# The expert stage of a two-block transformer kernel as one flat stream of weight pieces

## The chip, the cores and the metric

One core of a Trainium2 chip runs the whole program. The metric is the device time of one execution in microseconds (us), taken as the median of several executions.

## What is computed

Two stacked blocks on 256 tokens of width 1024 (x is 1 x 256 x 1024, float32). The first has two hybrid attention layers, the second has two hybrid mixers (a gated convolution and a delta rule), one behind each a feed-forward part: a dense SwiGLU of width 2816 after the first mixer, and a mixture of experts after the second. The change touches the mixture of experts alone:

```python
def moe_swiglu(x, router_w, w_gate, w_up, w_down):
    logits = (x @ router_w).astype(jnp.float32)
    top_v, top_i = lax.top_k(logits, TOP_K)              # TOP_K = 2 of N_EXPERTS = 8
    gates = jax.nn.softmax(top_v, axis=-1)
    combine = jnp.sum(jax.nn.one_hot(top_i, N_EXPERTS) * gates[..., None], axis=-2)
    y = jnp.zeros_like(x)
    for e in range(N_EXPERTS):
        y = y + combine[..., e:e + 1] * swiglu(x, w_gate[e], w_up[e], w_down[e])
    return y                                             # swiglu: (silu(x @ wg) * (x @ wu)) @ wd
```

The experts are 3584 wide, so gate, up and down weights of all eight are 352 MB, and each is read once.

## The kernel before

Every engine runs its own program, and they meet at semaphores. Up to the last mixer the order is a list of named jobs; the expert stage behind it (`experts` on PE, ACT and DVE, the loop over pieces on SP) is written out by hand.

**Items.** The router gives each expert the tokens that chose it. An item is an expert with at most 128 of its tokens; in this run there are 8 items, one for each expert, and a hardware loop on each engine goes over them. For an item PE gathers the tokens with a one-hot matrix `pick` into banks 4 and 5 (`gather`, L1325), and at its end spreads the result over all tokens with the weighted transpose `pickT` (the scatter, L1418 to L1421); `turn_picks` (L1334) makes that transpose, and DVE adds the four scattered halves into `total` (L2414). With `n` the item, the gather in iteration `n` is the one of item `n + 1`, so the last iteration gathers for nothing.

**Pieces.** The weights of an item come in 42 pieces of 1 MB, each 128 x 2048 float32: 28 gate and up pieces (seven chunks q of 512 columns, each with two gate and two up pieces), then 14 down pieces. A product is taken as three products of rounded numbers, hi x hi, hi x lo and lo x hi. So ACT rounds each piece into another slot (`piece_hi`, L1439, a helper's line for all its copies), and DVE writes raw minus hi over the raw piece (L2393, `piece_lo`). There are 7 slots for raw and lo, and 7 for hi. ACT's copy waits for the load alone, since with 7 and 7 a hi slot is free whenever its raw slot could be loaded again. SP loads a piece (L703) once the piece 7 earlier is used up (`piece_used`). PE makes 12 matmuls for a piece (L1394 to L1396 for gate and up, L1409 for down), 128 x 512 each.

**Order within an item.** PE makes all seven gate and up chunks first, into banks 0 and 1 or 2 and 3 by turns. Behind a chunk's up pieces ACT takes silu (L1714), DVE multiplies (L2401), PE transposes the hidden chunk (`turn_hidden`, L1372, behind the following chunk), ACT rounds it (`he_hi`) and DVE takes the rest (`he_lo`). Only then come the 14 down pieces into banks 6 and 7, the gather of the next item, the copy of the result to `ye` by ACT, the scatter and `turn_picks`. The first gate piece of the next item needs `xe_ready` and `lo_ready`; DVE handles gathered tokens, then the four additions, then the first `lo`:

```python
evacuate(n + 1)                       # DVE: xe_hi, xe_lo of the next item
...
tt(total[:, i, cs], total[:, i, cs], bank[b][:, :], ALU.add).then_inc(S("acc_added"), 1)
```

"Seam" below is the time between the last down piece of an item and the first gate piece of the next.

Of the kernel before, what the change touches and what calls it, by code (L numbers as in the profile page):

```python
# [8 lines left out]
P = 128  # L9
D = 1024  # L10
T = 256
NT = T // P
KD = D // P
# [45 lines left out]
NE = 8  # L59
# [3 lines left out]
RING = 5  # L63
# [6 lines left out]
NPIECE_UP = 4 * NQ  # L70
NPIECE = NPIECE_UP + D_FE // 256
MOE_RING = 7
FAR = 1e4

# [256 lines left out]
def build(nc, A, out_dram):  # L331
# [65 lines left out]
    with ctx:  # L397
# [128 lines left out]
        more_his = sb("more_his", [P, 2 * MOE_RING - 2 * RING, PIECE], fp32r)  # L526


        xe_hi, xe_lo = sb("xe_hi", [P, KD, P], fp32r), sb("xe_lo", [P, KD, P], fp32r)
        he_hi, he_lo = sb("he_hi", [P, KE, P], fp32r), sb("he_lo", [P, KE, P], fp32r)  # L530
        hse, ht = (uT[:, 4 * n:4 * n + 4, :].rearrange("p k t -> p (k t)").rearrange("p (a f) -> p a f", a=2) for n in range(2))
# [43 lines left out]
        piece_loaded = [S(f"piece_loaded{n}") for n in range(MOE_RING)]  # L575
# [9 lines left out]
        def half_slot(memory, j, p):  # L585

            if j < 2 * RING:
                flat = memory[:, (first_ring + j // 2) % RING, j % 2 * PIECE:(j % 2 + 1) * PIECE]
            else:
                flat = more_his[:, j - 2 * RING, :]  # L590
            return flat.rearrange("p (k n) -> p k n", n=FE_PART if p < NPIECE_UP else D)

        def piece_raw(p):

            return half_slot(ring, p % MOE_RING, p)

        def piece_lo(p):

            return half_slot(ring_r, p % MOE_RING, p)

        def piece_hi(p):

            return half_slot(ring_r, MOE_RING + p % MOE_RING, p)
# [27 lines left out]
        def _(sp):  # L631
# [63 lines left out]
            def load_piece(p, e):  # L695
                if p < NPIECE_UP:
                    q, side, half = p // 4, p % 4 // 2, p % 2
                    src = A["moe_w_up_2" if side else "moe_w_gate_2"][0]
                    src = src[e, 512 * half:512 * half + 512, q * FE_PART:(q + 1) * FE_PART]
                else:  # L700
                    r = (p - NPIECE_UP) * 256
                    src = A["moe_w_down_2"][0][e, r:r + 256, :]
                sp.dma_start(piece_raw(p), src.rearrange("o (k p) n -> p (o k) n", p=P)).then_inc(piece_loaded[p % MOE_RING], 16)  # L703

            for p in range(NPIECE):
                if p < MOE_RING:
                    slot_free(sp, loads[len(loads) - RING + p // 2][0])
                else:
                    sp.wait_ge(S("piece_used"), p - MOE_RING + 1)
                load_piece(p, bass.ds(0, 1))  # L710
                if p == MOE_RING - 1:
                    norm_rows(sp, NORMS - 1, A["ln_ffn_g_2"][1], A["ln_ffn_b_2"][1])
            sp.wait_ge(S("items_ready"), 1)
            nitems = sp.value_load(items[0:1, 4 * NE:4 * NE + 1], min_val=NE, max_val=2 * NE - 1)
            with sp.Fori(1, nitems) as n:
                e = sp.value_load(items[0:1, bass.ds(n + 2 * NE, 1)], min_val=0, max_val=NE - 1)
                for p in range(NPIECE):
                    sp.wait_ge(S("piece_used"), n * NPIECE + (p - MOE_RING + 1))
                    load_piece(p, bass.ds(e, 1))
# [6 lines left out]
        def _(pe):  # L726
# [598 lines left out]
            def gather():  # L1325

                for half in range(2):
                    for f in range(4):
                        for i in range(NT):
                            last = mm(bank[4 + half][:, f * P:(f + 1) * P], x[:, i, (4 * half + f) * P:(4 * half + f + 1) * P],  # L1330
                                      pick[:, i, :], start=(i == 0), stop=(i == NT - 1))
                    last.then_inc(S("gathered"), 1)

            def turn_picks():  # L1334

                for i in range(NT):
                    last = nc.tensor.transpose(bank[6][:, i * P:(i + 1) * P], pickc[:, i, :], C("ident"))
                last.then_inc(S("picks_full"), 1)

            def experts():  # L1340
# [21 lines left out]
                gather()  # L1362
                turn_picks()
                pe.wait_ge(S("items_ready"), 1)
                nitems = pe.value_load(items[0:1, 4 * NE:4 * NE + 1], min_val=NE, max_val=2 * NE - 1)
                def turn_hidden(n, q):

                    pe.wait_ge(S("hidden"), n * NQ + (q + 1))
                    if q >= 2:
                        pe.wait_ge(S("he_ready"), n * NQ + (q - 1))  # L1370
                    for f in range(4):
                        last = nc.tensor.transpose(bank[4 + q % 2][:, f * P:(f + 1) * P], ht[:, q % 2, f * P:(f + 1) * P], C("ident"))  # L1372
                    last.then_inc(S("hidden_turned"), 1)

                def split_ready(n, p):

                    pe.wait_ge(S("lo_ready"), n * NPIECE + (p + 1))
                    return piece_hi(p), piece_lo(p)


                with pe.Fori(0, nitems) as n:
                    pe.wait_ge(S("xe_ready"), n * 2 + 2)
                    for q in range(NQ):
# [14 lines left out]
                        if q:  # L1398
                            turn_hidden(n, q - 1)
# [1051 lines left out]
```

## Time and profile before

| | |
|---|---|
| runs | 2308.01, 2296.75, 2308.5 us; median 2308.01 |
| profiled execution | 2311.72 us, its span 2309.9 us |
| mean granted clock of TensorE | 0.939 of full |
| PE busy | 2140.4 us (93%), 10310 matmuls |
| DVE, ACT busy | 1512.7 us (65%), 968.1 us (42%) |
| all DMA | 502.07 MB, mean 217 GB/s over the span |
| chain that ended last | PE 86%, DVE 11% of the span |
| first expert matmul / span's end | 1264.07 / 2309.9 us |

PE is TensorE's matmuls, PEld its weight loads, DVE VectorE, ACT ScalarE, SP the engine that issues the loads; a name with q at its end is an engine's sequencer. A matmul's record is longer than the distance to the next one's start, because matmuls are pipelined; distances of starts tell the pace.

### The profile page before, as it was taken

The numbers are of one execution on the slowest core, as the hardware profiler recorded it, in microseconds if no ns is written. First come the engines' busy times: TensorE is split into PE (matmuls) and PEld (weight loads), VectorE is DVE, ScalarE is ACT, GpSimd is POOL, SyncE is SP. The second block draws the span as 40 slices with busy tenths as digits, with TensorE's granted clock in tenths as the row PEclk, the third lists the DMA queues.
The fourth block names the chain that finished last, engine by engine and source line by source line (L and its number), as shares of the span: only waits on it lengthen the run. The fifth ranks groups of instructions, "written<-read, shape, count | busy, mean of one in ns | idle before, by whom it ended". The sixth has DMA issues, their size and how long they took to land.

```text
span 2309.9 us, 27160 instructions
## 1 busy us (share of the span) xinstructions
PE 2140.4 (93%) x10310; PEld 1694.0 (73%) x10310; DVE 1512.7 (65%) x1786; ACT 968.1 (42%) x1043; POOL 153.8 (7%) x178
## 2 busy tenths in 40 slices
PE   7999989998969799989587999999999999999997
PEld 4776566765848499878475887878787887878786
DVE  4464424444395455429745879978787879978786
ACT  1102301122123244312232766757575766767573
POOL 0000000000352000008010000000000000000000
PEclk9987989789988899999697999999999999999999
DMA  9861034511530255454101998989898998989894
GB/s 336 280 212 43 28 118 137 184 37 37 196 118 1 73 165 183 164 169 145 37 1 38 371 375 301 369 313 370 302 371 299 374 368 304 372 304 367 304 369 159
DMA packets 238686, 502.07 MB, mean 217 GB/s; under 512 B 11258, under 2 KB 53010, under 8 KB 238610
## 3 DMA queue, kind: packets, MB, share of 16 engines
q1 hardware_dynamic: 238610, 501.03, 60.5%
q8 instruction: 51, 0.84, 0.1%
q14 instruction: 25, 0.20, 0.0%
HBM read 499.96 MB, written 1.05 MB: 217 GB/s over the span
## 4 chain that ended last, share of the span: by engine, by line
PE 86%; DVE 11%; issue 1%; ACT 1%; DMA 0%; DVEq 0%; SPq 0%; ACTq 0%
PE bank L1409 13%; PE bank L1394 9%; PE bank L1396 9%; PE bank L1395 9%; PE bank L737 7%; DVE cacc L2148 4%; PE bank L1098 3%; PE bank L982 3%; PE bank L938 3%; PE bank L1123 3%; PE bank L1310 3%; PE bank L744 3%; PE bank L1274 3%; PE bank L1077 2%; PE bank L1293 2%; PE bank L1295 2%
## 5 line engine op out<-in xcount | busy, mean ns | idle before, releaser
L2393 DVE TENSOR_TENSOR ring_r<-ring,more_his 128x2048 fp32r<-128x2048 f32 x192 | 433.6, 2287 | 10.6 <-ACT more_his L1439 10.4
L1439 ACT ACTIVATE more_his<-ring 128x2048 fp32r<-128x2048 f32 x192 | 358.9, 1908 | 13.5 <-DMA ring<-in_moe_w_down_dram 13.2
L1395 PE MATMUL bank<-ring_r,xe_hi 128*128 128x512 f32 x896 | 353.3, 394 | 0.0
L2393 DVE TENSOR_TENSOR ring_r<-ring,ring_r 128x2048 fp32r<-128x2048 f32 x144 | 325.3, 2287 | 24.9 <-ACT ring_r L1439 24.7
L1439 ACT ACTIVATE ring_r<-ring 128x2048 fp32r<-128x2048 f32 x144 | 268.0, 1908 | 3.8 <-DVE items L2360 3.8
L1394 PE MATMUL bank<-more_his,xe_hi 128*128 128x512 f32 x512 | 201.6, 394 | 0.0
L1396 PE MATMUL bank<-more_his,xe_lo 128*128 128x512 f32 x512 | 199.7, 390 | 0.0
L1395 PEld LDWEIGHTS bank<-ring_r,xe_hi 128*128 128x128 f32 x896 | 171.2, 191 | 34.8
L1409 PE MATMUL bank<-ring_r,he_hi 128*128 128x512 f32 x640 | 182.6, 391 | 0.0
L1394 PE MATMUL bank<-ring_r,xe_hi 128*128 128x512 f32 x384 | 156.5, 408 | 23.1 <-DVE ring_r L2393 23.1
L737 PE MATMUL bank<-uT,ring 128*128 128x256 f32 (+3 forms) x640 | 153.4, 399 | 4.1 <-DVE uT L1890 2.7
L1396 PE MATMUL bank<-ring_r,xe_lo 128*128 128x512 f32 x384 | 154.1, 401 | 0.0
L1123 PE MATMUL bank<-uT,ring 128*128 128x256 f32 x640 | 146.2, 393 | 2.0 <-ACT uT L1439 2.0
L737 PEld LDWEIGHTS bank<-uT,ring 128*128 128x128 f32 (+3 forms) x640 | 119.4, 189 | 38.4 <-issue 13.3
L1123 PEld LDWEIGHTS bank<-uT,ring 128*128 128x128 f32 x640 | 126.3, 198 | 21.1 <-issue 2.7
L1409 PEld LDWEIGHTS bank<-ring_r,he_hi 128*128 128x128 f32 x640 | 119.5, 188 | 24.6
L1396 PEld LDWEIGHTS bank<-more_his,xe_lo 128*128 128x128 f32 x512 | 96.1, 188 | 20.4
L1394 PEld LDWEIGHTS bank<-more_his,xe_hi 128*128 128x128 f32 x512 | 96.1, 188 | 19.2
L1293 PE MATMUL bank<-uT_r,ff_hi 128*128 128x256 f32 x352 | 101.0, 287 | 3.8 <-DVE u_lo L2297 3.8
L1394 PEld LDWEIGHTS bank<-ring_r,xe_hi 128*128 128x128 f32 x384 | 74.7, 195 | 40.3 <-DVE ring_r L2393 25.0
L1294 PE MATMUL bank<-u_lo,ff_hi 128*128 128x256 f32 x352 | 100.8, 286 | 0.0
L1295 PE MATMUL bank<-uT_r,ring_r 128*128 128x256 f32 x352 | 100.8, 286 | 0.0
(421 smaller groups left out, 3386.5 us busy)
## 6 DMA issues: line engine op xcount, KB each, us to landing
ring<-in_moe_w_gate_dram SPq DMA_DIRECT2D x112, 1024.0 KB, 5.2
ring<-in_moe_w_up_dram SPq DMA_DIRECT2D x112, 1024.0 KB, 5.3
ring<-in_moe_w_down_dram SPq DMA_DIRECT2D x112, 1024.0 KB, 4.9
ring<-in_w_in_dram SPq DMA_DIRECT2D x16, 2048.0 KB, 8.5
ring<-in_w_ada_dram SPq DMA_DIRECT2D x12, 2048.0 KB, 8.7
ring<-in_w_out_dram SPq DMA_DIRECT2D x8, 2048.0 KB, 8.2
ring<-in_w_in_dram SPq DMA_DIRECT2D x10, 1536.0 KB, 7.3
ring<-in_ffn_w_gate_dram SPq DMA_DIRECT2D x11, 1024.0 KB, 5.3
```

The costliest lines, as they stand in the source:

```text
L737: last = mm(b[0:n, to:to + T], w[:, k, a:a + n], uT[:, k, :], start=(k == 0), stop=(k == KD - 1))
L1123: last = mm(b[:, f * T:(f + 1) * T], w[:, k, a:a + P], uT[:, k, :], start=(k == 0), stop=(k == KD - 1))
L1293: mm(o, hi[:, k, a], u_hi[:, k, :], start=(k == 0), stop=False)
L1294: mm(o, hi[:, k, a], u_lo[:, k, :], start=False, stop=False)
L1295: last = mm(o, lo[:, k, a], u_hi[:, k, :], start=False, stop=(k == KD - 1))
L1394: mm(b[:, :], xe_hi[:, k, :], hi[:, kk, :], start=(k == 0), stop=False)
L1395: mm(b[:, :], xe_hi[:, k, :], lo[:, kk, :], start=False, stop=False)
L1396: last = mm(b[:, :], xe_lo[:, k, :], hi[:, kk, :], start=False, stop=(k == KD - 1))
L1409: last = mm(bank[6 + c][:, :], a[:, k, :], w[:, kk, 512 * c:512 * c + 512], start=(k == 0 and a is he_hi and w is hi), stop=(k == KE - 1 a ...
L1439: return go(out, in_, ACT.Copy, scale=scale)
L2148: ins = stt(cacc[:, f, :], src, w, cacc[:, f, :], ALU.mult, ALU.add)
L2393: tt(piece_lo(p), piece_raw(p), piece_hi(p).bitcast(fp32), ALU.subtract).then_inc(S("lo_ready"), 1)
```

## The change

The stage is one stream of pieces. A chunk is now six pieces: two gate, two up, and the two down pieces of the chunk before. PE's order in a chunk is gate, `turn_hidden` of the chunk before, up, down of the chunk before. Chunk 5 of an iteration (counted from -2) is the first of the next item; there the down pieces come first, and the gather of the next item stands ahead of them, in two halves. The result of the old item is copied (`copy_out`) and scattered in chunk 6, between the gate, up and down pieces of the new one, into banks 5, 0, 1 and 5. `he_hi` and `he_lo` hold one chunk where they held seven.

The memory is divided anew: 14 slots for raw and lo (`RAWS`), 3 for hi (`HIS`). SP issues a load when the piece 14 earlier is used up. ACT's copy of piece s now also waits until PE has used piece s - 3. The rounding of gathered tokens (`xe_hi`) moves from DVE to ACT. The loop has one iteration less: chunks -2 and -1 stand before it, and the last item's chunks 0 to 4 with two down pieces and the scatter behind it. There is no gather without use, and `turn_picks` moves to chunk 0. DVE's four `total` products of the start move from ahead of the first `lo` to behind chunk -1, and the token picking of the next item moves to chunk 1.

```diff
+RAWS, HIS = 14, 3
+def chunk_at(j):
+    return {-2: 0, -1: 4}.get(j, HEAD + 6 * j)
...
 def experts():                                   # PE
+            def chunk(n, j):
+                s0, q, g = chunk_at(j), (j + 2) % NQ, n * NQ + (j + 2)
+                b = 2 * (q % 2)
+                if j == 0:
+                    pe.wait_ge(S("acc_added"), n * 4 + 4)
+                if j == 5:
+                    turn_hidden(g - 1)
+                    pe.wait_ge(S("picks_copied"), n + 1)
+                    pe.wait_ge(S("picked"), n + 2)
+                    gather(0)
+                    pe.wait_ge(S("he_ready"), g)
+                    gather(1)
+                    down_pieces(n, g - 1, s0)
+                    s0 += 2
+                if q == 0:
+                    pe.wait_ge(S("xe_ready"), n * 2 + (4 if j == 5 else 2))
+                up_pieces(n, s0, b)
+                if j > -2 and j != 5:
+                    turn_hidden(g - 1)
+                if j == 0:
+                    turn_picks()
+                if j == 6:
+                    pe.wait_ge(S("ye_copied"), n + 1)
+                    for at, to in enumerate((5, 0, 1)):
+                        scatter(n, at, to)
+                up_pieces(n, s0 + 2, b + 1)
+                if j == 6:
+                    pe.wait_ge(S("acc_added"), n * 4 + 5)
+                    scatter(n, 3, 5)
+                if j > -2 and j != 5:
+                    down_pieces(n, g - 1, s0 + 4)
...
+                def split_hi(n, s, first=False):     # ACT
+                    act.wait_ge(piece_loaded[s % RAWS], n * (16 * NPIECE // RAWS) + 16 * (s // RAWS + 1))
+                    if not (first and s < HIS):
+                        act.wait_ge(S("piece_used"), n * NPIECE + (s - HIS + 1))
+                    copy(piece_hi(s), piece_raw(s)).then_inc(S("hi_ready"), 1)
...
+                    for r in range(4 if j == -2 else 6):   # ACT, chunk(n, j)
+                        split_hi(n, s0 + r, first=j < 0)
+                        if j > -2 and r == (1 if j == 5 else 3):
+                            hidden_hi(g - 1)
+                        if j == 5 and r == 1:
+                            gathered_hi(n + 1)
+                        if j == 5 and r == 4:
+                            copy_out(n)
+                        if r == {-2: 3, 5: 5}.get(j, 4):
+                            gate_silu(n, j)
...
+                    for r in range(4 if j == -2 else 6):   # DVE, chunk(n, j)
+                        split_lo(n, s0 + r)
+                        if j > -2 and r == (1 if j == 6 else 0):
+                            gated(n, g - 1, j - 1)
+                        if j > -2 and r == (1 if j == 5 else 3):
+                            hidden_lo(g - 1)
+                        if j == 5 and r == 1:
+                            gathered_lo(n + 1)
+                        if j == 6 and r == 4:
+                            for at, b in enumerate((5, 0, 1)):
+                                add_out(n, at, b)
+                        if j == 6 and r == 5:
+                            add_out(n, 3, 5)
...
-                sp.wait_ge(S("piece_used"), n * NPIECE + (p - MOE_RING + 1))
+                sp.wait_ge(S("piece_used"), n * NPIECE + (s - RAWS + 1))
```

ACT, in the middle of an item. Before (`more_his` and `ring_r` are hi slots, `he_hi` the rounded hidden chunk, `uT` the silu):

```order
L1439 ACTIVATE more_his<-ring 128x2048 [waits piece_loaded3]
L1439 ACTIVATE more_his<-ring 128x2048 [waits piece_loaded4]
L1717 REGISTER_ALU
L1439 ACTIVATE he_hi<-bank 128x512 [waits hidden_turned]
L1439 ACTIVATE more_his<-ring 128x2048 [waits piece_loaded5]
L1439 ACTIVATE more_his<-ring 128x2048 [waits piece_loaded6]
L1713 REGISTER_ALU
L1714 ACTIVATE uT<-bank 128x512 [waits piece_used]
```

The same engine after the change, from the fourth piece of a chunk on (`his` are the three hi slots):

```order
L1765 REGISTER_ALU [waits piece_loaded11]
L1497 ACTIVATE his<-more_raw 128x2048 [waits piece_used]
L1777 REGISTER_ALU
L1497 ACTIVATE he_hi<-bank 128x512 [waits hidden_turned]
L1765 REGISTER_ALU [waits piece_loaded12]
L1497 ACTIVATE his<-more_raw 128x2048 [waits piece_used]
L1784 ACTIVATE uT<-bank 128x512 [waits piece_used]
L1765 REGISTER_ALU [waits piece_loaded13]
L1497 ACTIVATE his<-more_raw 128x2048 [waits piece_used]
```

Each copy of a piece now waits for `piece_used` too, and in every chunk one copy stands behind that of `he_hi`, which waits for PE's transposes.

PE, at the end of the loop's body before: gather, scatter and `turn_picks` stand in a row behind the last down piece, and the branch back follows:

```order
L1409 MATMUL bank<-more_his,he_lo 128x512 x2
L1414 REGISTER_ALU
L1330 MATMUL bank<-pick,x 128x128 [waits picked]
L1330 MATMUL bank<-pick,x 128x128 x15
L1420 MATMUL bank<-ye,pickT 128x512 [waits ye_copied]
L1420 MATMUL bank<-ye,pickT 128x512 x3
L1337 MATMUL bank<-const,pickc 128x128 x2
L1381 REGISTER_ALU
L1381 COMPARE_AND_BRANCH
```

PE after the change, at the start of chunk 5, where the next item begins (L1371 transposes, L1357 is the gather, L1404 a down piece):

```order
L1369 REGISTER_ALU
L1371 MATMUL bank<-const,uT 128x128 [waits hidden]
L1371 MATMUL bank<-const,uT 128x128 x3
L1417 REGISTER_ALU
L1418 REGISTER_ALU [waits picks_copied]
L1357 MATMUL bank<-pick,x 128x128 [waits picked]
L1357 MATMUL bank<-pick,x 128x128 x7
L1357 MATMUL bank<-pick,x 128x128 [waits he_ready]
L1357 MATMUL bank<-pick,x 128x128 x7
L1398 REGISTER_ALU [waits he_ready]
L1404 MATMUL bank<-his,he_hi 128x512 [waits lo_ready]
```

The gather stands ahead of two down pieces, and its second half waits for `he_ready`, that is for ACT and DVE to empty the bank that the transposes just filled.

PE, at the end of the loop's body after the change, behind the last down piece of chunk 6:

```order
L1404 MATMUL bank<-his,he_lo 128x512 x2
L1470 REGISTER_ALU
L1470 COMPARE_AND_BRANCH
L1414 ISA
L1383 ISA [waits acc_added]
L1387 MATMUL bank<-his,xe_hi 128x512 [waits lo_ready]
L1388 MATMUL bank<-more_raw_r,xe_hi 128x512
```

No gather or scatter is left beside the branch; the branch lies between two pieces of the stream, and what follows it in the print is the last item's part. The scatter (L1376) has gone up between the pieces of chunk 6.

## Rows read from the trace of the kernel before

**Rows 1.** Windows: us, busy us (x instructions) of each engine, PEclk, DMA share, GB/s; expert stage

```profile
1264.07:2309.90 1045.83, 1012.48 (x4592) 829.16 (x4592) 873.82 (x557) 680.07 (x470) 0.00 (x0) 0.98 0.90 331
```

**Rows 2.** Windows: first gate matmul to last down matmul of items 2, 3 and 8

```profile
1393.64:1513.02 119.38, 119.38 (x532) 98.59 (x533) 100.89 (x59) 76.74 (x52) 0.00 (x0) 0.99 0.97 353
1523.17:1640.96 117.79, 117.79 (x533) 97.46 (x534) 100.71 (x59) 76.76 (x52) 0.00 (x0) 1.00 0.98 358
...
2169.11:2288.51 119.40, 119.40 (x533) 98.58 (x533) 100.89 (x59) 76.73 (x52) 0.00 (x0) 0.99 0.84 307
```

**Rows 3.** Waits in the expert stage: us in total, times, longest us

```profile
PE bank L1394 <- DVE ring_r L2393: 23.1, 8, 3.7
ACT more_his L1439 <- DMA ring<-in_moe_w_down_dram: 13.2, 17, 1.3
```

**Rows 4.** Timeline of PE, seam behind item 1: start, us, line, operation [idle before]

```profile
1383.49 3.73 PE L1330 MATMUL bank<-pick,x 128*128 128x128 f32 x32
1387.06 3.60 PE L1420 MATMUL bank<-ye,pickT 128*128 128x512 f32 x8
1390.49 0.38 PE L1337 MATMUL bank<-const,pickc 128*128 128x128 f32 x2
1393.64 0.50 PE L1394 MATMUL bank<-ring_r,xe_hi 128*128 128x512 f32 x1 [2.77 <-DVE ring_r L2393]
```

**Rows 5.** Timeline of DVE, the same seam

```profile
1390.70 0.69 DVE L2414 TENSOR_TENSOR total<-total,bank 128x512 f32<-128x512 f32 x1 [0.17 <-PE bank L1420]
1391.30 6.69 DVE L2393 TENSOR_TENSOR ring_r<-ring,ring_r 128x2048 fp32r<-128x2048 f32 x3
```

**Rows 6.** Windows: behind that seam, the stretch at a lower granted clock

```profile
1394.90:1398.21 3.31, 3.31 (x10) 2.53 (x8) 3.31 (x3) 0.00 (x1) 0.00 (x0) 0.52 0.00 0
```

**Rows 7.** Timeline within item 1: starts of two pieces four apart; transposes and ACT's copy

```profile
1274.02 0.39 PE L1394 MATMUL bank<-more_his,xe_hi 128*128 128x512 f32 x1
...
1284.90 0.39 PE L1394 MATMUL bank<-ring_r,xe_hi 128*128 128x512 f32 x1
...
1298.99 0.60 PE L1372 MATMUL bank<-const,uT 128*128 128x128 f32 x4
1299.62 0.60 ACT L1439 ACTIVATE he_hi<-bank 128x512 fp32r<-128x512 f32 x1 [1.67 <-PE bank L1372]
```

**Rows 8.** The page's costliest groups: ACT's hi copies, DVE's lo subtractions

```profile
L2393 DVE TENSOR_TENSOR ring_r<-ring,more_his 128x2048 fp32r<-128x2048 f32 x192 | 433.6, 2287 | 10.6 <-ACT more_his L1439 10.4
L1439 ACT ACTIVATE more_his<-ring 128x2048 fp32r<-128x2048 f32 x192 | 358.9, 1908 | 13.5 <-DMA ring<-in_moe_w_down_dram 13.2
```

**Rows 9.** Loop's line on PE's sequencer, first seam; instruction queue over the expert stage

```profile
L1381 PEldq COMPARE_BRANCH  x1: 252/252/252, 1386.3 to 1386.3; - x1
L1381 PEldq FUSED_REGOPS  x1: 50/50/50, 1386.6 to 1386.6; - x1
q8 instruction: 5, 0.08, 0.0%
```

**Rows 10.** Windows: 100 us within item 1; item 2 with its seam

```profile
1280.00:1380.00 100.00, 100.00 (x456) 82.76 (x455) 85.95 (x48) 67.68 (x46) 0.00 (x0) 1.00 1.01 373
1393.64:1523.17 129.53, 126.77 (x574) 103.78 (x574) 108.44 (x69) 85.94 (x60) 0.00 (x0) 0.99 0.93 340
```

**Rows 11.** Timeline of ACT, DVE and PE at the stage's start

```profile
1253.12 5.51 ACT L1439 ACTIVATE ring_r<-ring 128x2048 fp32r<-128x2048 f32 x3 [3.82 <-DVE items L2360]
1254.11 1.43 DVE L2386 TENSOR_SCALAR total<-x 128x512 f32<-128x512 f32 x4
1260.16 0.69 DVE L2378 CAST xe_hi<-bank 128x512 fp32r<-128x512 f32 x1 [0.61 <-PE bank L1330]
1264.07 0.50 PE L1394 MATMUL bank<-ring_r,xe_hi 128*128 128x512 f32 x1 [3.73 <-DVE ring_r L2393]
```

**Rows 12.** Timeline of ACT and PE behind the last down piece of item 8

```profile
2288.71 1.09 ACT L1439 ACTIVATE ye<-bank 128x512 f32<-128x512 f32 x2 [11.55 <-PE bank L1409]
2292.08 0.59 PE L1420 MATMUL bank<-ye,pickT 128*128 128x512 f32 x1
```

More of the change, by code:

```diff
@@ L705, in _, with load_piece @@
[L705 to L711, printed above, removed]
+            def load_piece(s, e):
+                what, _, q, half = piece_of(s)
+                if what == "d":
+                    r = 512 * q + 256 * half
+                    src = A["moe_w_down_2"][0][e, r:r + 256, :]
+                else:
+                    src = A["moe_w_up_2" if what == "u" else "moe_w_gate_2"][0]
+                    src = src[e, 512 * half:512 * half + 512, q * FE_PART:(q + 1) * FE_PART]
+                sp.dma_start(piece_raw(s), src.rearrange("o (k p) n -> p (o k) n", p=P)).then_inc(piece_loaded[s % RAWS], 16)
@@ L1323, in dense, with gather @@
                         down(n, [i])
[L1325 to L1332, printed above, removed]
+            def gather(half):
+                for f in range(4):
+                    for i in range(NT):
+                        last = mm(bank[5 - half][:, f * P:(f + 1) * P], x[:, i, (4 * half + f) * P:(4 * half + f + 1) * P],
+                                  pick[:, i, :], start=(i == 0), stop=(i == NT - 1))
+                last.then_inc(S("gathered"), 1)
@@ L1361, in experts @@
                 pe.wait_ge(S("picked"), 1)
-                gather()
-                turn_picks()
+                gather(0)
+                gather(1)
                 pe.wait_ge(S("items_ready"), 1)
[L1365 to L1373, printed above, removed]
@@ new lines, in experts @@
+                more = pe.value_load(items[0:1, 4 * NE:4 * NE + 1], min_val=NE - 1, max_val=2 * NE - 2)
+                chunk(0, -2)
+                chunk(0, -1)
+                with pe.Fori(0, more) as n:
+                    for j in range(NQ):
+                        chunk(n, j)
+                n = more
+                for j in range(5):
+                    chunk(n, j)
+                turn_hidden(n * NQ + 6)
+                down_pieces(n, n * NQ + 6, chunk_at(5))
+                pe.wait_ge(S("ye_copied"), n + 1)
@@ L1424, in _ @@
+                for at in range(4):
+                    scatter(n, at, at)
             mixer(0)
@@ new lines, in experts @@
+                chunk(0, -2)
+                chunk(0, -1)
+                with act.Fori(0, more) as n:
+                    for j in range(NQ):
+                        chunk(n, j)
+                n = more
+                for j in range(5):
+                    chunk(n, j)
+                for r in range(2):
+                    split_hi(n, chunk_at(5) + r)
+                hidden_hi(n * NQ + 6)
+                act.wait_ge(S("piece_used"), n * NPIECE + NPIECE)
+                copy(ye[:, 0:512], bank[6][:, :])
@@ L1723, in experts @@
+                copy(ye[:, 512:D], bank[7][:, :]).then_inc(S("ye_copied"), 1)
                 norm_scale(NORMS - 1)
@@ L2415, in experts @@
-                dve.wait_ge(S("acc_added"), nitems * 4 + 4)
+                with dve.Fori(0, more) as n:
+                    for j in range(NQ):
+                        chunk(n, j)
+                n = more
+                for j in range(5):
+                    chunk(n, j, last_item=True)
+                s, g = chunk_at(5), n * NQ + 6
+                split_lo(n, s)
+                gated(n, g, 4)
+                split_lo(n, s + 1)
+                hidden_lo(g)
+                for at in range(4):
+                    add_out(n, at, at)
```

261 lines of the change are left out of this document (136 added, 125 removed).

## The prediction

> **What bounds the kernel now.** I first split the span at the first expert matmul. The expert stage is 1045.8 of 2309.9 us; its DVE is busy 874 us and its ACT 680, PE 1012 [rows 1]. Nothing ahead of it changes. Next, the windows from the first gate matmul to the last down matmul of each item: PE is busy for the whole of each, and the lengths are 119.31 to 119.42 us for seven items and 117.79 for the third; three of the eight stand in [rows 2]. So inside an item no other engine is late. The waits agree: PE waits for DVE 8 times, once for each item, 23.1 us in all, and ACT waits for loads 13.2 us without PE noticing [rows 3]. The loss is at the seams, and the timeline of one shows what it consists of: gather 3.57 us, scatter 3.43, `turn_picks` 0.38, then PE idle 2.77, until DVE has made the first `lo` [rows 4]. DVE had the last addition to do first, which stands ahead of that `lo` in its queue [rows 5]. 1.3 us after PE resumes, matmuls go at a granted clock of 0.52, about the 1.2 GHz level, for 3.3 us [rows 6]. Item 3 is the one with PEclk 1.00 throughout, which prices this drop at 119.36 - 117.79 = 1.57 us [rows 2].
>
> **Time base.** The sum is made against the profiled execution, 2311.72 us (span 2309.9 and 1.8 around it). The median of the runs is 3.7 us lower, 2308.0; I apply the same difference to it. One of the three runs was 2296.75, so a level may shift by 11 us without any change.
>
> **Units of the stream.** Four pieces are 1284.90 - 1274.02 = 10.88 us, one is 2.72 [rows 7]. An item without a clock drop is 42 x 2.72 = 114.2, which leaves 3.6 for seven `turn_hidden`, 0.51 each [rows 2]. ACT's hi copy takes 1.91 and DVE's subtraction 2.29 us [rows 8]; in a row they follow at (5.51 - 1.91) / 2 = 1.80 and (6.69 - 2.29) / 2 = 2.20 [rows 5, 11]. ACT starts 0.20 behind the start of PE's next work (2288.51 to 2288.71) [rows 2, 12]. From the end of a `lo` to PE is 1393.64 - 1391.30 - 2.29 = 0.05 [rows 4, 5]; I take the same from ACT to DVE.
>
> **Three hi slots.** The new wait makes every piece go round a loop: PE ends piece s - 3, ACT copies s, DVE subtracts, PE may start s. From the start of piece s - 2 that is 0.20 + 1.91 + 0.05 + 2.29 + 0.05 = 4.50 us, and PE wants s after two pieces, 5.44. Cover 0.94. The tight place is the first down piece of a chunk, whose copy stands behind that of `he_hi`. Count from a chunk's start: two gate pieces, 5.44; transposes; `he_hi` starts 0.63 behind them (1298.99 to 1299.62) [rows 7], 6.07 to 6.67; then 1.91 + 0.05 + 2.29 + 0.05 gives 10.97. PE gets there at 5.44 + 0.51 + 5.44 = 11.39. Cover 0.42 us, so no stall. DVE's other work (multiply, `he_lo`, picks) lies in gaps: it issues six subtractions in 13.2 of a chunk's 16.8 us. ACT has more room. Price of this part: 0; if the cover goes, PE stalls 56 times (rival 2).
>
> **Seams.** Removed: 7 idles of 2.77, 19.4 us, and the six clock drops behind seams, 6 x 1.57 = 9.4 (the one at the stage's start stays). Gather, scatter and `turn_picks` are only moved. Added: the gather's second half waits for `he_ready`. The turn is 0 to 0.51, the first half to 2.30; `he_hi` is done at 1.23, but DVE is in a subtraction until about 1.9 (that piece's copy could start only at the use of the piece three before it), then `he_lo` takes some 0.69 like the other 512-column operation [rows 5]. So PE waits until 2.65, 0.35 x 7 = 2.5 us. Two more changes of shape inside a stream, taken at 0.1 each, 0 to 0.3 by what is left over for a turn [rows 2, 7]: 1.4. In chunks 5 and 6 I walked the three queues in the same way: the two `ye` copies (1.09 [rows 12]) delay ACT's last copy of chunk 5 and leave 0.7, the three additions leave over 1 us. Nothing stalls, and they are late nowhere else: `piece_used`, `ye_copied` and `acc_added` come before PE asks.
>
> **Start.** Before, DVE did `total`, tokens, then the first `lo`. After, two `lo` lie under the gather: ACT's copies run from 1253.12 [rows 11]. The last half of the tokens was gathered at 1260.16; ACT 0.60, DVE 0.69 and hops let PE start at 1261.6 and not 1264.07: 2.4 us gained. The four `total` products (1.43 us [rows 11]) come between chunk -1 and chunk 0, against a cover of 0.9: 1 us back.
>
> **End.** The useless gather had hidden the `ye` copies: 2288.51 to 2292.08, 3.57 us [rows 2, 12]. Now the last two down pieces wait for `he_lo`, 2.65 - 0.51 = 2.1, and the copies are bare, 0.20 + 1.09 + 0.05 = 1.3. Net 0.1 gained, taken as 0.
>
> **Loads.** 42 pieces are 44.04 MB. The new item takes 117.8 + 3.6 + 3.4 + 0.4 + 0.35 + 0.2 = 125.7 us, so 350 GB/s; the queues gave 373 for 100 us while saturated [rows 10]. With 14 slots a load has over 25 us to land. 0. SP only waits at other counts.
>
> **Sum.** -19.4 - 9.4 + 2.5 + 1.4 - 2.4 + 1.0 = -26.3, say -26. Profiled: 2311.7 - 26 = 2286. Median: 2308.0 - 26 = **2282 us** (-1.1%).
>
> **Rivals.**
> 1. *The clock still falls at the seams.* PE idles 0.35 us there, in the middle of 7 us of small float32 matmuls. Against it: gathers and scatters ran at PEclk 1.00 before, and what preceded the drops was the idle 2.77; that seam 2 kept the clock with the same idle says it is marginal. It gives back 9.4 + 1.6: 2293. The Trainium skill says under "TensorE: Matmul & The Clock Gate", A second HAM failure mode, that a kernel which idles briefly between groups can oscillate between clocks; no row here shows it for idles this short.
> 2. *Slower: the hi slots bind.* Place: the first down piece of each of 56 chunks, whose copy waits for `he_hi`. If the loop is longer than my rows by 0.42 us PE begins to stall, at 0.89 (0.47 x 56 = 26) the gain is gone, at 1.3 it is 0.88 x 56 = 49 us, so -26 + 49 = +23, 2331. For it: ACT waited for transposes and PE waited on nobody before, since 7 slots gave it distance; matmul ends are modelled. Against: both copies are steady (the groups' means, rows 8, hold over 192), and the hop behind a matmul was seen.
> 3. *The branch in mid-stream.* Before, the branch back was hidden in the seam. At most the idle of 2.77 hid it: 7 x 2.77 = 19.4, so 2301. Against: PE's sequencer took 0.25 us for the branch, the next register operation followed at once, and that was 4 us before the queued matmuls ended; the queue of instructions moved 5 packets in the whole stage [rows 9]. The Trainium skill ("Runtime: NRT & Kernel Launch", Instruction fetch mechanics) says that a taken branch to code that is not held forces a fetch and a stall, which speaks against this change; 8 iterations with 5 packets do not agree for these loops.
> 4. *Loads bind.* If the rate over an item were the 340 GB/s of before [rows 10], an item would stay at 129.5: 7 x 3.8 = 27 back, 2309. But that 340 has a seam in it in which SP had no free slot.
>
> **How the numbers follow.** My case 0.70; rival 1 0.11 (0.08 of it below the bound), rival 2 0.10 (0.08 slower, 0.02 same), rival 3 0.05 (same), rival 4 0.04 (0.03 same, 0.01 slower). The bound is 0.5%, 11.5 us, about what a measurement of this kernel can tell: faster is below 2296.5. Faster 0.78, same 0.13, slower 0.09. My case alone runs from 2277 (nothing added: -31) to 2290 (stalls of 0.15 us in each chunk, +8), and down to 2268 if the level of the lowest run shows. To hold 8 in 10 the range takes in rivals 1 and 3: 2268 to 2303.
>
> **What would show it.** Right: from item to item 125.5 to 126 us; PE's waits for DVE a few tenths at each chunk 5 and none elsewhere; PEclk 1.00 from the second item on; no PE wait at `lo` in mid-chunk; DMA about 350 GB/s. Wrong: idles of PE before the first down piece (rival 2), at the branch between chunks 6 and 0 (rival 3), a clock of 0.5 behind the gather (rival 1), ACT waiting for `ring` or `more_raw` loads (rival 4).

## The result and the profile after

The changed kernel takes **2271.25 us** (median of 4 runs, 2269.55 to 2275.37); the kernel before, run beside it, 2304.83 (4 runs, 2296.75 to 2308.5). The ratio is 0.986, 95% interval [0.983, 0.989]: faster by 1.4%. A second series of the same kernel on the chip of the last experiments gave 2270.97 against 2306.17, ratio 0.987 [0.983, 0.991]. Forecast were 2282 and a ratio of 0.989.

The two profiled executions are 2311.72 and 2275.37 us, 36.3 apart, and that is more than the change did. Here is TensorE up to the first expert matmul, its timeline before and then after (start, us, line, operation, idle before and its releaser):

```profile
1238.26 6.97 PE L1347 MATMUL bank<-router_w,uT 128*128 128x8 f32 x32 [0.99 <-ACT uT L1439]
1254.34 5.79 PE L1330 MATMUL bank<-pick,x 128*128 128x128 f32 x32 [4.51 <-DVE pickc L2368]
```

```profile
1232.55 6.97 PE L1449 MATMUL bank<-router_w,uT 128*128 128x8 f32 x32 [0.99 <-ACT uT L1497]
1248.64 5.23 PE L1357 MATMUL bank<-pick,x 128*128 128x128 f32 x32 [4.51 <-DVE pickc L2471]
1255.28 0.50 PE L1387 MATMUL bank<-his,xe_hi 128*128 128x512 f32 x1 [1.41 <-DVE xe_lo L2486]
```

The router's text is the same in both and it starts 5.7 us earlier. The windows from 1030 to 1050 us show one place where this comes from, before and after (us, busy us of each engine, granted clock, DMA share, GB/s):

```profile
1030.00:1050.00 20.00, 20.00 (x94) 17.64 (x93) 8.36 (x17) 2.21 (x6) 9.96 (x13) 0.83 0.35 124
```

```profile
1030.00:1050.00 20.00, 20.00 (x109) 17.78 (x109) 9.67 (x20) 2.71 (x7) 10.01 (x12) 1.00 0.35 128
```

Both are code that the change didn't touch. Over all kernels of this study the router starts anywhere from 1226.5 to 1238.3 us. So from here on I measure the **stage**: from the start of the first gather to the start of the last scatter.

| kernel | gather | first expert matmul | last scatter | stage |
|---|---|---|---|---|
| before | 1254.34 | 1264.07 | 2292.08 | 1037.7 |
| after | 1248.64 | 1255.28 | 2255.61 | 1007.0 |

The stage gained 30.8 us. Behind the last scatter both take 18. The kernel before was traced in one execution only; how many seams drop the clock in its other executions isn't shown. The windows after, in the same columns: first expert matmul to the gather of item 2, one item from gather to gather, the last gather to the last scatter, and 3 us out of that last stretch:

```profile
1255.28:1368.58 113.30, 112.97 (x510) 92.92 (x511) 99.20 (x61) 80.92 (x53) 0.00 (x0) 1.00 0.98 356
1368.58:1493.80 125.22, 125.15 (x576) 102.73 (x575) 108.55 (x67) 89.29 (x61) 0.00 (x0) 1.00 0.97 352
2119.81:2255.61 135.80, 132.63 (x600) 108.25 (x598) 109.67 (x64) 91.01 (x65) 0.00 (x0) 0.99 0.67 245
2249.00:2252.00 3.00, 3.00 (x10) 2.33 (x9) 0.00 (x0) 0.00 (x0) 0.00 (x0) 0.55 0.00 0
```

An item is 125.2 us, was 129.53 [rows 10], and TensorE is busy for all but 0.07 of it; the granted clock is 1.00 in every item. It falls once, near 1.2 GHz, at the very end. The waits of TensorE, the matmuls' and then the weight loads', answer to [rows 3]; 23.1 us in 8 waits are gone:

```profile
PE bank L1404 <- DVE he_lo L2498: 1.9, 1, 1.9
PE bank L1387 <- DVE xe_lo L2486: 1.4, 1, 1.4
PE bank L1376 <- ACT ye L1497: 1.2, 1, 1.2
PE bank L1387 <- DVE ring_r L2478: 0.3, 1, 0.3
...
PEld bank L1357 <- DVE he_lo L2498: 1.8, 7, 0.3
```

Each of the first four occurs once: `xe_lo` ahead of the first expert matmul, `ring_r` in chunk -1, `he_lo` and `ye` at the end. The last is the price of the new place of the gather, 0.26 us in each of seven items. The seam of [rows 4] now looks like this:

```profile
1368.15 0.60 PE L1371 MATMUL bank<-const,uT 128*128 128x128 f32 x4
1368.58 4.07 PE L1357 MATMUL bank<-pick,x 128*128 128x128 f32 x32
1372.41 0.70 PE L1404 MATMUL bank<-his,he_hi 128*128 128x512 f32 x2
```

A gather, 3.83 us from start to the next piece against 3.57, and nothing idle behind it. The end of the stage, the counterpart of [rows 12]:

```profile
2244.57 0.60 PE L1371 MATMUL bank<-const,uT 128*128 128x128 f32 x4
2247.09 0.72 PE L1404 MATMUL bank<-his,he_hi 128*128 128x512 f32 x2 [1.93 <-DVE he_lo L2498]
...
2249.65 1.06 PE L1404 MATMUL bank<-more_raw_r,he_hi 128*128 128x512 f32 x2
...
2253.83 0.61 PE L1404 MATMUL bank<-his,he_lo 128*128 128x512 f32 x2
2255.61 3.70 PE L1376 MATMUL bank<-ye,pickT 128*128 128x512 f32 x8 [1.17 <-ACT ye L1497]
```

After the transposes TensorE idles 1.93 us, then two matmuls take 1.06 where they take 0.62 elsewhere: the clock dropped behind that idle.

The hi loop is the subject of rival 2. VectorE's timeline in one chunk of item 2, and TensorE's starts of the pieces that wait for these `lo` (1442.96 is the chunk's first gate piece; the transposes and two up pieces follow, then the first down piece):

```profile
1439.67 2.29 DVE L2478 TENSOR_TENSOR ring_r<-ring,his 128x2048 fp32r<-128x2048 f32 x1 [0.42 <-ACT his L1497]
...
1451.47 4.58 DVE L2478 TENSOR_TENSOR more_raw_r<-more_raw,his 128x2048 fp32r<-128x2048 f32 x2 [0.75 <-ACT his L1497]
```

```profile
1442.96 0.39 PE L1387 MATMUL bank<-his,xe_hi 128*128 128x512 f32 x1
...
1448.40 0.60 PE L1371 MATMUL bank<-const,uT 128*128 128x128 f32 x4
...
1454.09 0.39 PE L1389 MATMUL bank<-his,xe_lo 128*128 128x512 f32 x1
```

The ordinary `lo` ends at 1441.96 and its piece starts at 1442.96: 0.95 us of cover behind the 0.05 for the hop. The tight one ends at 1451.47 + 2.29 = 1453.76, its piece starts one matmul (0.22) behind 1454.09, at 1454.31: 0.50.

### The profile page after: what moved, and what is told of

Same layout as the page of the kernel before. It is cut to its first block, busy times and chain, and to the rows that moved or that the text cites. A ratio compares the mean times of both kernels' runs of the same rounds, so it can differ in the third digit from the quotient of the medians.

```text
span 2273.6 us, 27344 instructions
## 1 busy us (share of the span) xinstructions
PE 2121.1 (93%) x10276; PEld 1676.3 (74%) x10276; DVE 1508.6 (66%) x1762; ACT 994.8 (44%) x1059; POOL 153.8 (7%) x178
## 4 chain that ended last, share of the span: by engine, by line
PE 84%; DVE 12%; issue 2%; ACT 2%; DMA 0%; DVEq 0%; SPq 0%; ACTq 0%
PE bank L1404 12%; PE bank L1387 9%; PE bank L1389 9%; PE bank L1388 9%; PE bank L765 7%; DVE cacc L2251 4%; PE bank L1126 3%; PE bank L1010 3%; PE bank L966 3%; PE bank L1151 3%; PE bank L1302 3%; PE bank L1338 3%; PE bank L772 3%; PE bank L1105 2%; PE bank L1321 2%
## 5 line engine op out<-in xcount | busy, mean ns | idle before, releaser
L2478 DVE TENSOR_TENSOR ring_r<-ring,his 128x2048 fp32r<-128x2048 f32 x240 | 548.8, 2290 | 84.9 <-ACT his L1497 84.8
L1497 ACT ACTIVATE his<-ring 128x2048 fp32r<-128x2048 f32 x240 | 460.1, 1918 | 136.0 <-PE bank L1389 78.9
L1387 PE MATMUL bank<-his,xe_hi 128*128 128x512 f32 x896 | 356.0, 397 | 1.7 <-DVE xe_lo L2486 1.4
L1389 PE MATMUL bank<-his,xe_lo 128*128 128x512 f32 x896 | 349.5, 390 | 0.0
L1388 PE MATMUL bank<-ring_r,xe_hi 128*128 128x512 f32 x704 | 274.0, 389 | 0.0
L2478 DVE TENSOR_TENSOR more_raw_r<-more_raw,his 128x2048 fp32r<-128x2048 f32 x96 | 219.8, 2291 | 32.2 <-ACT his L1497 32.1
L1497 ACT ACTIVATE his<-more_raw 128x2048 fp32r<-128x2048 f32 x96 | 184.2, 1918 | 57.4 <-PE bank L1404 31.9
L1387 PEld LDWEIGHTS bank<-his,xe_hi 128*128 128x128 f32 x896 | 168.3, 188 | 37.7 <-issue 1.7
L1389 PEld LDWEIGHTS bank<-his,xe_lo 128*128 128x128 f32 x896 | 168.2, 188 | 35.8
L1404 PE MATMUL bank<-his,he_hi 128*128 128x512 f32 x448 | 142.3, 399 | 1.9 <-DVE he_lo L2498 1.9
L1404 PE MATMUL bank<-his,he_lo 128*128 128x512 f32 x448 | 138.8, 391 | 0.0
L1404 PEld LDWEIGHTS bank<-his,he_hi 128*128 128x128 f32 x448 | 84.1, 189 | 22.1 <-issue 3.4
```

The lines of the kernel that those rows point to most:

```text
L1387: mm(bank[b][:, :], xe_hi[:, k, :], hi[:, kk, :], start=(k == 0), stop=False)
L1388: mm(bank[b][:, :], xe_hi[:, k, :], lo[:, kk, :], start=False, stop=False)
L1389: last = mm(bank[b][:, :], xe_lo[:, k, :], hi[:, kk, :], start=False, stop=(k == KD - 1))
L1404: last = mm(bank[6 + c][:, :], a[:, k, :], w[:, kk, 512 * c:512 * c + 512], start=(q == 0 and k == 0 and a is he_hi and w is hi), stop=(q ...
L1497: return go(out, in_, ACT.Copy, scale=scale)
L2478: tt(piece_lo(s), piece_raw(s), piece_hi(s).bitcast(fp32), ALU.subtract).then_inc(S("lo_ready"), 1)
```

## Experiments

### Is the flat stream needed, or only its look-ahead?

My theory: the gain is the covered seam, nothing else. The kernel before, with its order of gate, up and down pieces and 7 slots, but ScalarE and VectorE two pieces ahead across the seam:

```diff
+AHEAD = 2
...
-                with act.Fori(0, nitems) as n:
-                    for p in range(NPIECE):
+                for p in range(AHEAD):
+                    act.wait_ge(piece_loaded[p], 16)
+                    copy(piece_hi(p), piece_raw(p)).then_inc(S("hi_ready"), 1)
+
+                def item(n, ahead):
+                    for p in range(AHEAD, NPIECE + ahead):
...
+                with act.Fori(0, more) as n:
+                    item(n, AHEAD)
+                item(more, 0)
```

and the same on VectorE, where the two `lo` come before the emptying of the gather's banks.

> The kernel before, with one thing changed: ACT rounds and DVE splits pieces 0 and 1 of the next item before DVE handles the gathered tokens and the additions (the loop over pieces runs from 2 to 43, the last item apart). Order of PE, 7 and 7 slots, gather and scatter at the seam stay. Theory (the gain is the seam's idle 2.77 us and the clock drop it causes, and the flat order only a way to cover it): from item to item 117.79 + 3.57 + 3.43 + 0.38 = 125.2 us against 129.5 before and 125.2 after; the start gains about 1.2; the stage 29 to 32 us shorter than before, the same as after within 3 us. Rival (it takes the gather and scatter inside a stream, with down pieces one chunk behind, to be rid of the idle or the clock drop): PEclk falls behind some seams, item to item 126.8 or more where it does, at least 10 us slower than after.

2270.52 us (4 runs, 2263.71 to 2278.31), before 2301.24; ratio 0.986 [0.981, 0.990]. One seam on TensorE, and one item in the windows:

```profile
1376.90 3.73 PE L1331 MATMUL bank<-pick,x 128*128 128x128 f32 x32
1380.47 3.60 PE L1421 MATMUL bank<-ye,pickT 128*128 128x512 f32 x8
1383.91 0.38 PE L1338 MATMUL bank<-const,pickc 128*128 128x128 f32 x2
1384.05 0.48 PE L1395 MATMUL bank<-ring_r,xe_hi 128*128 128x512 f32 x1
```

```profile
1384.04:1508.93 124.89, 124.89 (x577) 102.63 (x576) 108.46 (x68) 86.20 (x59) 0.00 (x0) 1.00 0.96 353
```

The idle of 2.77 is gone and so is the clock drop behind it; the item is 124.89 us, 0.3 shorter than in the flat stream, which pays 0.26 for `he_ready`. The stage is 1004.0 us against 1007.0. The stage is 33.7 us shorter than before, a little more than the 29 to 32 expected, because the item came out at 124.89 and not 125.2. The expectation had an item of before less its idle and its clock drop, 129.53 - 2.77 - 1.57 = 125.19; the 0.30 that is left is what a restart behind an idle costs beyond the idle itself (the run with extra copies shows 0.28 at another place). So the seam was the whole prize, and the order inside an item, the 14 slots and the split hi slots carried none of it.

### What is left if the gather isn't covered

In the flat stream, the two down pieces of chunk 5 move ahead of the gather (and ScalarE and VectorE handle the gathered tokens two pieces later):

```diff
+                    down_pieces(n, g - 1, s0)
                     gather(0)
-                    pe.wait_ge(S("he_ready"), g)
                     gather(1)
-                    down_pieces(n, g - 1, s0)
```

> The changed kernel with one move: in chunk 5 the two down pieces stand ahead of the gather, so that nothing of PE lies between the gather and the first gate piece of the new item (ACT and DVE handle the gathered tokens behind the fourth piece of the chunk). PE must idle for xe_hi and xe_lo, 0.20 + 0.60 + 0.05 + 0.69 = about 1.5 us, and loses the wait of 0.26 for he_ready. Theory that an idle of this size does not lower the clock: item to item 125.2 + 1.2 = 126.4, PEclk 1.00. Rival (any idle beside the gather lowers the clock): a stretch at 0.5 behind it and 128.0.

2300.88 us (one run), stage 1038.2; from gather to gather 128.97 us, and 130.57 where the clock drops between them. My expectation, 126.4 at a clock of 1.00, was short: I had reckoned with the bare `xe_lo` and overlooked that the gather also covers `he_lo`. The first two seams:

```profile
1365.16 1.02 PE L1404 MATMUL bank<-his,he_hi 128*128 128x512 f32 x2 [2.04 <-DVE he_lo L2497]
1372.34 3.73 PE L1357 MATMUL bank<-pick,x 128*128 128x128 f32 x32
1377.56 0.49 PE L1387 MATMUL bank<-his,xe_hi 128*128 128x512 f32 x1 [1.49 <-DVE xe_lo L2485]
...
1495.73 0.73 PE L1404 MATMUL bank<-his,he_hi 128*128 128x512 f32 x2 [2.04 <-DVE he_lo L2497]
1501.30 3.73 PE L1357 MATMUL bank<-pick,x 128*128 128x128 f32 x32
1506.53 0.49 PE L1387 MATMUL bank<-his,xe_hi 128*128 128x512 f32 x1 [1.49 <-DVE xe_lo L2485]
```

Two idles of 2.04 and 1.49 in place of one of 0.26. Behind the 1.49, the idle that the expectation was about, the clock stayed up at all seven seams; it fell behind the other one. The two pieces behind the first take 1372.34 - 1365.16 = 7.18 us at seam 1 and 5.57 at seam 2: the same idle dropped the clock at seams 1, 3 and 5 and not at the four others, at 1.6 us each. That is the price of 1.57 which the prediction read off [rows 2]. The sum: 7 x (3.53 - 0.26) = 22.9 for the idles and 3 x 1.6 = 4.8 for the clock. 31.2 were measured, which leaves 3.5, or 0.5 a seam, for the two restarts. This last figure is what is left over and not a separate reading, but it is near twice the 0.28 of the next experiment.

### The hi slots and their margin

Two hi slots in place of three (the first rounding of gathered tokens moves one piece ahead with it); and, separately, three slots with two more copies of 512 columns on ScalarE behind `he_hi`, which nothing reads, in six of the seven chunks of each item:

```diff
-RAWS, HIS = 14, 3
+RAWS, HIS = 14, 2
```

```diff
                             hidden_hi(g - 1)
+                            if j != 5:
+                                for t in range(2):
+                                    copy(spare[:, t, :], x[:, 0, 0:512])
```

> The changed kernel with 2 hi slots in place of 3 (14 raw slots kept). The loop PE end of piece s - 2, copy, subtraction, PE start of s then binds every piece. If the loop is the 4.50 us worked out from rows of before, a piece takes 4.50 and not 2.72 us, and the stage is 336 x 1.78 = 598 us longer, somewhat less or more for the transposes that fall into the idle or into the loop. If semaphores or queues cost more when they bind than when they are slack, the piece takes over 4.7 us. Either way it gives the loop's length, which sets the cover of 3 slots.

> The changed kernel with two further ACT copies of 128 x 512 (about 0.5 us each, into a spare tile that nothing reads) behind the copy of he_hi in six of seven chunks: 1.0 us more in the tight place. With the cover of 0.42 us of the prediction PE idles 0.6 us before the first down piece of each such chunk, 48 x 0.6 = 28 us; with the 0.50 us read in the trace of after (lo ends 1453.76, PE starts the piece at 1454.31) 24 us. If the cover were larger than 1.0 nothing happens. If short idles in mid-stream lower the clock, it is over 50 us.

Two slots: 2574.48 us (one run), stage 1312.1, +305. The size was misread, by me: I had one loop for each piece, but with two slots TensorE still has a piece between, so two pieces share a loop. Its starts behind the stalls:

```profile
1572.32 0.50 PE L1387 MATMUL bank<-his,xe_hi 128*128 128x512 f32 x1 [1.61 <-DVE ring_r L2478]
1579.67 0.50 PE L1387 MATMUL bank<-his,xe_hi 128*128 128x512 f32 x1 [1.59 <-DVE ring_r L2478]
```

7.35 us for two pieces here and 7.36 in the mean, so the loop is 7.36 - 2.72 = 4.64, where the prediction had 4.50 by its parts. (3.68 - 2.72) x 336 = 323 if every piece were bound by it; the chunks' gathers, scatters and transposes give some back. By this loop the cover of three slots would be 5.44 - 4.64 = 0.80 and not the 0.95 read in the trace after; why, is left open. Without the third slot the new order is 12% slower than the kernel before. Six clock drops of some 1.6 us each are in the +305; all come with idles of 2.2 us, none with the 1.6 above (the last section has them).

The extra copies: 2301.19 us (one run), stage 1032.0, +25.0. TensorE at two chunks:

```profile
1461.47 0.74 PE L1405 MATMUL bank<-his,he_hi 128*128 128x512 f32 x2 [0.36 <-DVE more_raw_r L2482]
...
1478.99 0.73 PE L1405 MATMUL bank<-his,he_hi 128*128 128x512 f32 x2 [0.39 <-DVE ring_r L2482]
```

The stall comes at the place that rival 2 named, the first down piece. A chunk is 1478.99 - 1461.47 = 17.52 us and without the copies 16.8, so each short stall of 0.38 costs 0.65 to 0.7: about 0.16 of it is the tail of the matmul before, which the records count as busy, and 0.12 a slower first matmul (0.73 for two where 0.62 is usual). Two copies are 1.09 us [rows 12], and of them 0.38 + 0.16 = 0.54 reach TensorE, so 0.55 were covered. The trace after shows 0.50 and the prediction had 0.42.

That the total meets the 24 to 28 us expected is partly luck. The expectation had 48 stalls of 0.5 to 0.6 us. The trace has 41, one in every chunk with extra copies but the seven with the scatters between their pieces, and the table of waits gives them 13.8 us in all; but each costs about 0.28 more than it shows. The end has no clock drop in this run, which saves 1.6, and the gather at the start is 0.55 longer than in the changed kernel.

### Load distance

14 slots stay, but SyncE waits for the piece seven before:

```diff
+DIST = 7
...
-                    sp.wait_ge(S("piece_used"), n * NPIECE + (s - RAWS + 1))
+                    sp.wait_ge(S("piece_used"), n * NPIECE + (s - DIST + 1))
```

> The changed kernel with its 14 raw slots, where SyncE issues a load when the piece seven before it has been used, in place of fourteen before: loads run at most as far ahead as with seven slots. If the second seven slots carry nothing of the gain (theory: a piece is used 2.79 us after the one before it and a load of 1 MB takes about 2.6 us of all queues, so seven pieces are 19 us of lead for a load that takes under 3), the pitch stays 125.2 us (to 125.5) and the stage 1007 us (to 1010). If the slots carry it (rival 4 of the prediction, loads bind), ScalarE waits for the load's landing, he and TensorE with it, some us in each item: a pitch of 128 us or more and a stage 20 us longer, likely with the clock at a half at some of the waits.

2275.68 us (one run), stage 1007.3:

```profile
1368.60:1493.86 125.26, 125.19 (x576) 102.74 (x575) 108.56 (x67) 89.28 (x61) 0.00 (x0) 1.00 0.96 352
```

TensorE and ScalarE wait for no load in the stage. Seven slots of distance are enough for the stream too. That a load takes under 3 us, as the expectation says, was wrong: the trace after has 5.0 to 5.3 us from issue to landing (medians), and seven pieces at 2.72 us are 19.

### A version with both lessons, and the changed kernel again

The look-ahead kernel without TensorE's gather and `turn_picks` behind the last item, and with the first `lo` ahead of the emptying of the first gather's banks:

```diff
-                with pe.Fori(0, nitems) as n:
+                def item(n, final=False):
...
-                    pe.wait_ge(S("picked"), n + 2)
-                    gather()
+                    if not final:
+                        pe.wait_ge(S("picked"), n + 2)
+                        gather()
...
+                first_lo(0)
                 evacuate(0)
+                first_lo(1)
```

> The kernel before with the two pieces of look-ahead, and two more cuts: TensorE doesn't gather and turn picks for an item behind the last one, and VectorE makes the first lo half before it empties the first gather's banks rather than behind it. Theory: both cuts lie on the path and outside the item's loop, so the pitch stays 124.9 us, the start (gather's first matmul to the first expert matmul) goes from 8.48 to about 7.3 us, and the end loses the 2.2 us that the last gather and its transposes take on TensorE before its last pieces: gather to last scatter 1004.0 - 1.2 - 2.2 = 1000.6 us, some 6 us shorter than the changed kernel's 1007.0 and so 0.3% under it, little more than its measurement can tell. Rival: TensorE waits at the end for he_lo all the same, and the end gains under 1 us: 1002 to 1003.

> The changed kernel itself, run again beside the two others on the same chip. Router, norm and attention are the same text in all of these kernels, and the start of the router has so far stood anywhere from 1226.5 to 1238.3 us after the span's start. My theory has the stage alone as the change's work: from the gather's first matmul (L1381) to the last scatter's issue 1007 us again (1006 to 1008), a pitch of 125.2 us, a granted clock of 1.00 in the whole stage, wherever the router starts; the time 2262 to 2276 us, ratio to the kernel before 0.983 to 0.989. The rival, that part of the 31 us was luck of one execution, has a clock that falls at one seam or more, 1.6 us for each.

2265.53 us (4 runs, 2263.59 to 2266.63) against 2270.97 (2269.56 to 2279.89) for the changed kernel on the same chip; against the kernel before, 0.983 [0.980, 0.986]. The stages are 1001.7 and 1007.1 us. The intervals of the two ratios overlap; that it beats the changed kernel rests on the stages, 5.3 us apart, and on its four runs, which all lie below the four of the changed kernel. Its pitch is 124.89 and its end is this, with no wait for `he_lo` and no clock drop, against the 1.93 and 1.06 above:

```profile
2244.53 0.61 PE L1410 MATMUL bank<-ring_r,he_hi 128*128 128x512 f32 x2
2246.78 3.70 PE L1422 MATMUL bank<-ye,pickT 128*128 128x512 f32 x8 [1.18 <-ACT ye L1446]
```

In this order the last transposes are followed by the down pieces of chunks that are long ready. The end gained the 2.2 us expected of it. The start did not gain its 1.2. Its first gather, timeline and window:

```profile
1245.06 6.74 PE L1331 MATMUL bank<-pick,x 128*128 128x128 f32 x32 [4.71 <-DVE pickc L2384]
1253.49 0.49 PE L1395 MATMUL bank<-ring_r,xe_hi 128*128 128x512 f32 x1 [1.47 <-DVE xe_lo L2396]
```

```profile
1245.06:1251.00 5.94, 5.94 (x28) 5.94 (x29) 4.78 (x7) 4.17 (x3) 0.00 (x0) 0.50 0.00 0
```

The idle fell from 2.58 to 1.47, but the gather went at a granted clock of 0.50 for 6 us; in the kernel without the cut it took 5.69 us in all. The clock rose later in this execution and took back what the order gave.

The second trace of the changed kernel repeats the first, as expected: a stage of 1007.1, an item of 125.21 us at a clock of 1.00, the drop at the end again, the router at 1228.11.

## Why the prediction was right, step by step

The sum was -26.3; the stage shows -30.8. By its terms:

| step | forecast | measured |
|---|---|---|
| idle at seven seams | -19.4 | -19.4 |
| restarts behind these idles | 0 | -2.0 |
| six clock drops behind them | -9.4 | -9.4 |
| clock drop at the stage's start | 0 | -1.6 |
| wait for `he_ready`, 7 times | +2.5 | +1.8 |
| two more changes of shape an item | +1.4 | +0.4 |
| start | -2.4 | -3.1 |
| `total` products | +1.0 | 0 |
| stall in chunk -1 | 0 | +0.6 |
| end | 0 | +1.5 |

These make -31.2; 0.4 of loss is spread over the stage in parts that I can't assign. The restarts are seven items of before less their idles and clock drops against those of the look-ahead kernel; the changes of shape are the flat stream's item less the 0.26 against the same.

The median, 2271.25, lies in the range, but below 2277, where my case alone was to end: the restarts, the drop at the stage's start and part of the start's gain were left out, the starting value was too high, and what the end lost did not make up for them.

**Seams and clock.** Right, and they are the result. The Trainium skill's rule, weighed at rival 1, of a kernel that idles briefly between groups and oscillates between clocks ("TensorE: Matmul & The Clock Gate", A second HAM failure mode), agrees with what was removed: behind idles of 2.77 us the clock fell at 6 of 7 seams, behind 2.04 at 3 of 7. No drop followed the idles that took their place, 0.26 us an item.

**Restarts.** A term that the prediction left out: an idle of 2.77 us was priced at 2.77, and each cost about 0.3 more. Most of it is the tail of `turn_picks`: I took it at its record, 0.38 us, but in the look-ahead kernel, where no idle follows, the next matmul starts 0.14 behind it (1383.91 to 1384.05). It is also half of why an item is 125.2 us and not the 125.7 forecast.

**Start.** I said that the drop at the stage's start stays. It went, together with most of the idle ahead of the first expert matmul, 3.73 and now 1.41 us [rows 11]. A mis-sized term, on the good side. The step from the gather to the first matmul went from 9.73 to 6.64 us. Of these 3.1 us 0.55 are luck of the clock: the same 32 matmuls of the gather took 5.79 us before and 5.23 after, because the clock stood at 0.50 for the first 4.1 us of them before and for 2.7 after. In the run with extra copies, whose start is the changed kernel's, they took 5.78 and the step 7.19: 2.5 gained, against 2.4 forecast.

**`total` products and chunk -1.** The products cost nothing: VectorE's next `lo` behind them ends at 1281.35 + 2.29 = 1283.64, and TensorE reaches its piece at 1283.75 without an idle. But TensorE stalls once inside chunk -1, at its second piece, where I had forecast nothing:

```profile
1269.53 0.50 PE L1387 MATMUL bank<-his,xe_hi 128*128 128x512 f32 x1 [0.33 <-DVE ring_r L2478]
```

```profile
1266.58 0.69 DVE L2493 TENSOR_TENSOR uT<-bank,uT 128x512 f32<-128x512 f32 x1 [0.78 <-PE bank L1389]
1281.35 2.29 DVE L2478 TENSOR_TENSOR more_raw_r<-more_raw,his 128x2048 fp32r<-128x2048 f32 x1
```

The multiplication of chunk -2 waits for the up piece just done and stands ahead of that `lo`. With the restart the 0.33 cost 0.6.

**End.** This step failed. I took the wait for `he_lo` (2.1, measured 1.93) and the bare `ye` copies (1.3, measured 1.33) against the 3.57 of the gather, and gave the clock no term. But 1.93 us of idle is of the kind that had dropped it at the seams, and it did, for 1.6 us: 1.93 + 1.33 + 1.62 - 3.57 = +1.3, and some 0.2 for the restart. The clock is the part that was missing.

**Hi slots.** Price 0, right. Cover 0.94 and 0.42 forecast, 0.95 and 0.50 read; the run with extra copies shows the stall at the place that the prediction named. Rival 2 priced a stall at its length alone, and each costs 0.28 more.

**Loads.** 0, right; 352 GB/s against the 350 worked out.

**Rivals.** 1 (clock still falls at the seams): in no item. 2 (hi slots bind): no wait for a `lo` inside a chunk but the one of 0.33 us in chunk -1, and the run with two slots shows what was at stake. 3 (branch in mid-stream): chunk 6 goes over into chunk 0 through the branch, and the matmuls are 0.23 us apart there as anywhere, in all seven passes. Timeline of TensorE after and its loop's line on the sequencer, which answers to [rows 9]:

```profile
1408.69 0.62 PE L1404 MATMUL bank<-his,he_lo 128*128 128x512 f32 x2
1409.14 0.39 PE L1387 MATMUL bank<-his,xe_hi 128*128 128x512 f32 x1
```

```profile
L1470 PEldq COMPARE_BRANCH  x7: 83/215/253, 1405.2 to 2156.4; - x7
```

The branch was decided at 1405.2, four microseconds ahead of the matmul that it leads to. Six of the seven are taken back, the last leaves the loop. The rule of a forced fetch and stall at a taken branch (the Trainium skill, "Runtime: NRT & Kernel Launch", Instruction fetch mechanics) cost nothing visible in them; it speaks of code that is not held, and whether this code was held no run here shows. 4 (loads bind): refuted twice, by ScalarE, which waits for no load in the stage, and by the shorter distance.

The forecast of the median was 11 us too high, of which the terms above explain 4.5. Of the rest, 3 us are the kernel before, whose median with a fourth run is 2304.83 where I started from 2308.0, and 3 us lie within what the unchanged part moves from one execution to the next.

## What to carry to other kernels

Where a loop's engines wait for each other only at its seam, let the feeding engines run two steps into the next round: that alone gave the whole gain here, and a new order of the entire stage gave no more. So try the small change first. Price an idle of TensorE together with the clock behind it, at the end of a stage as well as at the seams. And compare stages, not spans, when unchanged code ahead of the stage moves by 12 us.

## What the runs showed of the hardware

- Which idles drop the clock is not a matter of their length alone. 2.77 us, the seams of before: 6 of 7. 2.21, ahead of each item's last scatter in the run with two hi slots: 5 of 7. 2.04: 3 of 7. 1.93 at the stage's end: 4 of 4. 1.86 at the same place in the run with extra copies: not. 1.49 beside a bare gather: 0 of 7. 1.6 us every 7.4 us, in the run with two hi slots, left it at 1.00 over 290 us; the first drop of that run comes with a 2.21. Its windows and that idle:

```profile
1300.00:1590.00 290.00, 239.15 (x1023) 178.49 (x1024) 194.06 (x117) 159.71 (x109) 0.00 (x0) 1.00 0.80 273
1603.52:1606.90 3.38, 3.38 (x7) 2.13 (x8) 3.38 (x4) 0.00 (x0) 0.00 (x0) 0.56 0.66 271
```

```profile
1603.52 1.70 PE L1376 MATMUL bank<-ye,pickT 128*128 128x512 f32 x2 [2.21 <-DVE total L2506]
```

- A drop cost the same at the seams before, at those with the bare gather and at the stage's end: 1.57 to 1.62 us.
- A stall of 0.38 us costs 0.65 to 0.7. Behind the 2.77 us of the seams it is 0.3 more too. Many short waits cost more than their sum in the table of waits.
- The 1.8 us for `he_ready` stand only in the list of the weight loads' waits and not in that of the matmuls, so both have to be read.
